# Products of the identity in TensorE's idle stretches between the first projections and the experts

## The chip, the cores and the metric

The kernel runs on one core of a Trainium2 chip. The metric is the device time of one execution in microseconds (us). The engines are PE (TensorE: PE for its matmuls, PEld for its weight loads), DVE (VectorE), ACT (ScalarE), POOL (GpSimd) and SP (SyncE, which issues most of the DMAs).

## The reference, cut to what matters

The network has two blocks over 512 tokens of width 1024, all in float32. The first block ends in a mixture of experts: each token takes one of 4 groups, and 2 of the 8 experts of that group.

```python
g_logits = (t @ w_group + b_group)                     # 512 x 4
e_logits = einsum('td,gde->tge', t, w_expert) + b_expert   # 512 x 4 x 8
e_sel = e_logits of the group with the largest g_logit
top_vals, top_idx = lax.top_k(e_sel, 2)
gate = softmax(top_vals) * softmax(g_logits)[group]
act = silu(t @ w_gate_up[g, e, :, :256]) * (t @ w_gate_up[g, e, :, 256:])
y = sum over the chosen experts of gate * act @ w_down[g, e]
```

Ahead of it stand a projection (`proj = h @ w_in`), a causal attention, a spatial gating (`z = w_spatial @ layer_norm(gelu(vs))`) and an output projection with a layer norm. The second block (retention, state space, latent attention, two feed-forward layers) isn't touched.

## The kernel before, in words

Each engine has one program, a list of stages in fixed order (`tensor`, `scalar`, `vector`, `gpsimd`, `sync` at the end of `program`). Nothing is planned at run time: an engine runs its instructions in the order written and waits on semaphores (`wait_ge`) for what it needs from the others. TensorE's stages that matter here are `proj1_pe`, `attn1_pe`, `out1_pe`, `route_pe` and `experts_pe`, in this order. All matrices are cut in four blocks of 128 tokens, t = 0 to 3.

- `proj1_pe` (L642) makes the first projection with `proj3`, three products of rounded parts for each block, and near its end the spatial gating: `spatial(t)` is 8 products of a 128x128 matrix with 128x64 columns (`each`, L141), after `ln_dve` on DVE has made `vs_norm` of that block. At the end it makes the first scores of the attention (`scores1(p, 0)`), then `spatial(3)`; `attn1_pe` starts when DVE has used all four (`gated`).
- `out1_pe` (L867) is the output projection, 16 column groups of 8 products. Between these it takes each finished block: `turn(t)` makes 8 transposes (`turns`, L147) of the normalised rows, once DVE has made them (`h1`); ACT copies them to SBUF (`h1_T_copy`); `logits(t)` is 8 products with 36 columns (`acc`, L135). For the last blocks nothing is left to do between, so the order is `logits(2)`, `turn(3)`, `logits(3)`.
- `route_pe` (L978) sorts the tokens to experts. `route_dve` works out the choice in a chain of small instructions and raises `chosen`. TensorE then counts ranks (L982, L984: `ranks`), DVE works out the places (`selected`), TensorE makes the row numbers with 8 products of 48 columns (L135: `row_ids`), DVE converts them (`token_ids`), and POOL gathers the rows of the first tile by an indirect DMA (L1189).
- `experts_pe` (L1202 on) runs over 24 tiles of work: `rows(j)` makes 8 transposes of the gathered rows, which ACT and DVE copy; `up(j)` is 16 products of 512 columns (L1216), `down(j)` 8 (L1229). SP fetches the weights of tile n when tile n-2's `up` and `down` have freed their place (`expert_piece`, L1117 on, its DMAs at L1130): those of the first two tiles are there before, and the next fetch waits for the end of `up(0)`.

A semaphore is raised by the last product of a group, and what stands behind it in TensorE's list doesn't hold it back. PSUM has 8 banks; `bk(i, n)` is the first n columns of bank i.

Of the kernel before, what the change touches and what calls it, by code (L numbers as in the profile page):

```python
# [224 lines left out]
def program(nc, A, out):  # L225
    S = Sems(nc, FOLLOWS)
# [7 lines left out]
    def bk(i, n=512, at_=0):  # L234
        return PS[:, 512 * i + at_:512 * i + at_ + n]
# [23 lines left out]
    ident, ones, iot = C["ident"], C["ones"], C["iot"]  # L259
# [125 lines left out]
    def landed(x, n):  # L385

        x.wait_ge(S(f"piece{U[n]['slot']}"), U[n]["turn"])
        return cut(U[n], U[n]["raw"])
# [87 lines left out]
    def ada_pe(p, c):  # L476
        if c < 24:
            w, b, q = ada_weights(p, c), ada_bank(c // 12), c % 12
            p.wait_ge(S("bcol"), 1)
            for i in range(2):  # L480
                for j in range(4):
                    k = 2 * j + i
                    ins = p.e.matmul(PS[32 * j:32 * j + 32, 512 * b:512 * b + 512], cTv[:, k, 22 - 2 * q:54 - 2 * q], w[k // 4][:, k % 4, :],
                                     start=q == 0 and i == 0, stop=q == 11 and i == 1)
            p.up(ins, S("ada_row"))
        if c in (12, 24):
            p.wait_ge(S("ada_copy"), c // 12)
            p.each([(bk(ada_bank(c // 12 - 1), 24, 24 * b), arow[:, 128 * b:128 * b + 128], sel24[:, 0:24]) for b in range(4)], S("ada_T"))
# [137 lines left out]
    def proj3(p, n, t, bank, aH_, aL_, inc):  # L626
        wh, wl = parts(p, n)
        ts_ = slice(128 * t, 128 * t + 128)
        p.acc(bk(bank, 256), three([(aH_[:, k, ts_], aL_[:, k, ts_]) for k in range(8)],
                                   [(wh[:, k, :], wl[:, k, :]) for k in range(8)]), inc=inc)  # L630

    SCORE = (0, 1, 2, 7)

    def scores1(p, n):
        for m in (n, n + 1):
            h, t = units1[m]
            r0 = 64 * (h % 2)
            p.wait_ge(S("masked"), m - 3)
            p.each([(bk(SCORE[m % 4], 128 * t + 128), qT[r0:r0 + 64, h // 2, 128 * t:128 * t + 128],
                     kT[r0:r0 + 64, h // 2, 0:128 * t + 128])], inc=S("score"))  # L640

    def proj1_pe(p):  # L642
        p.wait_ge(S("x_low"), 8)

        def turn(i):
            p.wait_ge(S("roped1"), i + 1)
            p.wait_ge(S("qkT_copy"), i - 1)
            x = tmp[i % 2][:, 0:256]
            p.turns([(bk(6 + i % 2, 128, 128 * b), x[:, 128 * b:128 * b + 128]) for b in range(2)], ident, S("qk_T"))

        def spatial(t):
            p.wait_ge(S("vs_norm"), t + 1)
            p.wait_ge(S("gated"), t - 1)
            p.each([(bk(6 + t % 2, 64, 64 * g), wspT[:, g, :], vst[:, t, 64 * g:64 * g + 64]) for g in range(8)], inc=S("spatial"))

        for n in range(10):
            for t in range(4):
                g = 4 * n + t
                if g >= 4:
                    p.wait_ge(*((S("v_copy"), g - 3) if g < 12 else (S("act1"), g - 11)))  # L660
                proj3(p, W_IN[n], t, g % 4, xH, xL, S("proj1"))
                if n < 8 and t % 2:
                    ada_pe(p, g // 2)
                if 17 <= g < 33:
                    turn(g - 17)
                if g == 33:
                    p.wait_ge(S("wsp_m"), 1)
                    p.wait_ge(S("qkT_copy"), 16)
                    for h in range(2):
                        p.turns([(bk(6 + h, 128, 128 * j), wsp[:, 4 * h + j, :]) for j in range(4)], ident, S("wsp_T"))  # L670
                    p.wait_ge(S("wsp_copy"), 1)
                    p.turns([(bk(6, 8), X[0:8, 512:640])], ident, S("wsp_T"))
                    p.wait_ge(S("wsp_copy"), 3)
                if n == 9 and t:
                    spatial(t - 1)

        p.wait_ge(S("act1"), 31)
        scores1(p, 0)
        spatial(3)

    def proj1_act(a):
# [117 lines left out]
    def attn1_dve(v):  # L799
        c = 16  # L800
        for n in range(35):
            if n < 32:
# [5 lines left out]
                v.settle()  # L808
                v.stt(x[:, 0:w], bk(SCORE[n % 4], w), 0.125, lnc[:, t, 0:w], ALU.mult, ALU.add, inc=S("masked"))
                v.settle()  # L810
# [56 lines left out]
    def out1_pe(p):  # L867
        ada_pe(p, 24)
        p.wait_ge(S("o_copy"), 4)
        p.wait_ge(S("prob_T_copy"), 32)  # L870
        for k in range(4):
            p.wait_ge(S("mix_T_copy"), k - 2)
            p.turns([(bk((3, 5, 6)[k % 3], 128, 128 * t), mix1[:, t, 128 * k:128 * k + 128]) for t in range(4)], ident, S("mix_T"))
        p.wait_ge(S("mix_T_copy"), 4)

        def turn(t):
            p.wait_ge(S("h1"), t + 1)
            for b in range(2):
                p.wait_ge(S("h1_T_copy"), 2 * t + b - 1)
                p.turns([(bk(5 + b, 128, 128 * j), hl[:, t, 128 * (4 * b + j):128 * (4 * b + j) + 128]) for j in range(4)],  # L880
                        ident, S("h1_T"))

        def logits(t):
            p.wait_ge(S("h1_T_copy"), 2 * t + 2)
            p.wait_ge(S("logit"), t - 1)
            p.wait_ge(S("in3"), 176)
            p.acc(bk(3 + t % 2, 36), [(hT[:, k, 128 * t:128 * t + 128], wr[:, k, :]) for k in range(8)], inc=S("logit_m"))

        for c in range(2):
            w = [landed(p, W_O + 2 * c), landed(p, W_O + 2 * c + 1)]  # L890
            for t in range(4):
                g = 4 * c + t
                p.wait_ge(S("added1"), g - 2)
                p.acc(bk(g % 3), [(mT[:, k, 128 * t:128 * t + 128], w[k // 4][:, k % 4, :]) for k in range(8)], inc=S("out1"))
                if c and t >= 2:
                    logits(t - 2)
                if c and t:
                    turn(t - 1)
        logits(2)
        turn(3)  # L900
        logits(3)

    def out1_act(a):
        for k in range(4):
            a.wait_ge(S("mix_T"), k + 1)
            a.cast(mT[:, 4 + k, :], bk((3, 5, 6)[k % 3]), inc=S("mix_T_copy"))

        def copies(t):
            for b in range(2):
                a.wait_ge(S("h1_T"), 2 * t + b + 1)  # L910
                a.cast(hT[:, 4 * b:4 * b + 4, 128 * t:128 * t + 128], bk(5 + b).rearrange("p (k t) -> p k t", k=4), inc=S("h1_T_copy"))

        for t in range(4):
            if t:
                copies(t - 1)
            ln_act(a, LNS1)
        copies(3)
# [60 lines left out]
    def route_pe(p):  # L978

        p.wait_ge(S("chosen"), 1)  # L980
        tile = lambda q, n: v32(AS)[:, q, :].unsqueeze(1).to_broadcast([P, n, 32])
        p.e.matmul(bk(0, 160), C["U"], AS5, start=True, stop=False)  # L982
        for q in range(4):
            ins = p.e.matmul(bk(0, 160).rearrange("p (t n) -> p t n", t=5)[:, q + 1:5, :], ones, tile(q, 4 - q),  # L984
                             start=False, stop=q == 3)
        p.up(ins, S("ranks"))
        p.wait_ge(S("selected"), 1)
        p.acc(bk(1, 48), sel, inc=S("row_ids"))

    def route_act(a):  # L990
        answer(a, ge, ge, ACT.Exp)
        answer(a, dd, dd, ACT.Exp)
# [1582 lines left out]
    for l in range(2):  # L2575
        n = 0
# [393 lines left out]
    def tensor(e):  # L2970
        p = Lane(e, S("own_pe"))
        begin_pe(p)
        proj1_pe(p)
        attn1_pe(p)
        out1_pe(p)
        route_pe(p)
        experts_pe(p)
        qkv_pe(p)
        ret_pe(p)
        gnorm_pe(p)  # L2980
        conv_pe(p)
        ssd_pe(p)
        mix_pe(p)
        p.wait_ge(S("mixed_T_copy"), 16)
        ffn_pe(p, 0, aT, RWO, next_pe)
        latent_pe(p)
        heads_pe(p, 0)
        heads_pe(p, 1)
        p.wait_ge(S("o2_copy"), 32)
        p.wait_ge(S("exp2"), 64)  # L2990
        ffn_pe(p, 1, oT, MWO, nothing)
# [112 lines left out]
```

## Time and profile before

| | us |
|---|---|
| median of 3 runs | 2585.84 |
| the 3 runs | 2596.91, 2581.55, 2585.84 |
| time of the profiled execution | 2584.93 |
| its span in the trace | 2583.1 |
| TensorE's matmuls busy | 2427.2 |
| TensorE's weight loads busy | 1714.6 |
| DVE busy | 1144.3 |

The time of the profiled execution is its span and 1.8 us around it. All times in the rows below are microseconds from the start of the span, unless ns is written. A busy TensorE is one with a matmul under way, at whatever clock.

### The profile page before, as it was taken

The page shows a single profiled execution, that of the slowest core. Times are in us where ns is not written, and L with a number is a line of the kernel's source. Part 1 is how long each engine was busy: PE and PEld are TensorE (multiplying, and loading weights), DVE is VectorE, ACT ScalarE, POOL GpSimd, SP SyncE. Part 2 cuts the span into 40 slices and gives each one's busy share as a digit, 9 for nine tenths or more (in the row PEclk, how much of TensorE's full clock was granted, in tenths as well). Part 3 has the DMA queues.
Part 4 walks back from the last instruction along what each step waited for, and adds up shares of the span by engine and source line. Part 5 has one row for each costly group of instructions (what it writes and reads, how often), then busy time and mean ns, then how long its engine had stood idle before and what let it go on. Part 6 is the DMA issues. An engine that isn't in the chain of part 4 may idle for free.

```text
span 2583.1 us, 29977 instructions
## 1 busy us (share of the span) xinstructions
PE 2427.2 (94%) x12470; PEld 1714.6 (66%) x12470; DVE 1144.3 (44%) x1952; ACT 691.6 (27%) x1215; POOL 153.4 (6%) x147
## 2 busy tenths in 40 slices
PE   8998969999999998899999999999988999999998
PEld 6783433333445887747888888877756554788886
DVE  3247332111464666735443433443264473544444
ACT  2235012111133333314112112122253352322222
POOL 0000011111104104200000000000000000000000
PEclk9999969999999999999999999999999999999999
DMA  9937649998411510122112212112200101322222
GB/s 340 358 128 262 237 160 379 334 362 321 160 26 35 66 49 1 68 96 66 50 49 82 66 49 82 66 33 84 66 17 1 66 1 33 98 80 94 94 94 79
DMA packets 180039, 305.65 MB, mean 118 GB/s; under 512 B 18315, under 2 KB 89787, under 8 KB 179776
## 3 DMA queue, kind: packets, MB, share of 16 engines
q1 hardware_dynamic: 167792, 278.40, 31.8%
q0 software_dynamic: 11376, 23.17, 2.7%
q8 instruction: 99, 1.62, 0.3%
q10 hardware_dynamic: 736, 2.15, 0.2%
q14 instruction: 36, 0.29, 0.0%
HBM read 351.90 MB, written 18.90 MB: 144 GB/s over the span
## 4 chain that ended last, share of the span: by engine, by line
PE 61%; DVE 7%; ACT 3%; issue 2%; POOL 0%; DMA 0%; DVEq 0%; ACTq 0%
PE PS L135 37%; PE PS L2430 11%; PE PS L2374 4%; PE PS L141 3%; PE PS L147 3%; PE PS L2840 2%; DVE sm L116 1%; DVE X L105 1%; DVE H L105 1%; PE PS L2317 1%; DVE rest L105 1%; DVE MIX L105 1%; ACT ATb L128 1%; DVE H L113 1%; DVE R L113 0%
## 5 line engine op out<-in xcount | busy, mean ns | idle before, releaser
L135 PE MATMUL PS<-at,wH 128*128 128x512 f32 (+1 forms) x2144 | 563.2, 352 | 2.1 <-DVE at L105 2.1
L135 PEld LDWEIGHTS PS<-at,wH 128*128 128x128 f32 x2144 | 378.2, 189 | 56.9 <-DVE at L105 2.3
L135 PE MATMUL PS<-at,rest 128*128 128x512 f32 (+1 forms) x1072 | 376.3, 351 | 0.0
L2430 PE MATMUL PS<-wH,ac 128*128 128x512 f32 x880 | 277.8, 393 | 3.3 <-DVE hn L105 3.3
L105 DVE TENSOR_TENSOR rest<-ring,wH 128x2048 fp32r<-128x2048 f32 x66 | 150.4, 2291 | 211.1 <-ACT wH L128 210.5
L135 PEld LDWEIGHTS PS<-at,rest 128*128 128x128 f32 x1072 | 202.7, 189 | 27.0
L128 ACT CAST wH<-ring 128x2048 fp32r<-128x2048 f32 x66 | 124.6, 1906 | 272.1 <-PE PS L2430 199.8
L2430 PEld LDWEIGHTS PS<-wH,ac 128*128 128x128 f32 x880 | 165.2, 188 | 42.9 <-DVE hn L105 8.4
L2430 PE MATMUL PS<-rest,ac 128*128 128x512 f32 x440 | 171.4, 389 | 0.0
L135 PE MATMUL PS<-HI,ATr 128*128 128x256 f32 x512 | 150.0, 293 | 4.8 <-DVE MIXr L105 4.0
L135 PE MATMUL PS<-ring,AT 128*128 128x512 f32 x320 | 141.6, 599 | 0.8 <-ACT AT L128 0.8
L105 DVE TENSOR_TENSOR hn<-PS,gate 128x512 f32<-128x512 f32 x120 | 83.0, 692 | 104.4 <-PE PS L2430 99.3
L141 PE MATMUL PS<-R 96*128 96x256 f32 (+6 forms) x344 | 113.0, 488 | 14.9 <-DVE X L105 10.1
L105 DVE TENSOR_TENSOR sil<-sil,PS 128x512 f32<-128x512 f32 x66 | 39.5, 599 | 171.9 <-PE PS L135 171.8
L135 PEld LDWEIGHTS PS<-HI,ATr 128*128 128x128 f32 x512 | 100.3, 196 | 15.6 <-issue 10.8
L128 ACT COPY R<-PS 128x256 f32<-128x256 f32 (+4 forms) x148 | 65.6, 459 | 167.9 <-PE PS L135 139.1
L135 PEld LDWEIGHTS PS<-ring,AT 128*128 128x128 f32 x320 | 60.4, 192 | 74.2 <-issue 73.1
L135 PE MATMUL PS<-ring,X 128*128 128x256 f32 (+1 forms) x384 | 106.5, 433 | 1.3 <-ACT MIXb L128 1.3
L105 DVE TENSOR_TENSOR MIX<-MIX,PS 128x256 f32<-128x256 f32 (+1 forms) x34 | 15.9, 469 | 206.2 <-ACT MIX L125 205.3
L128 ACT CAST ac<-sil 128x1536 fp32r<-128x1536 f32 (+1 forms) x22 | 27.8, 1265 | 295.1 <-DVE sil L105 295.1
L2430 PEld LDWEIGHTS PS<-rest,ac 128*128 128x128 f32 x440 | 82.7, 188 | 17.0 <-issue 0.7
L147 PEld LDWEIGHTS PS<-con,R 128*128 128x128 f32 (+1 forms) x512 | 57.2, 137 | 55.0 <-issue 28.6
(332 smaller groups left out, 3896.7 us busy)
## 6 DMA issues: line engine op xcount, KB each, us to landing
R<-in_w_gate_up_dram SPq DMA_DIRECT2D x32, 1024.0 KB, 12.0
ring<-in_w_down_dram SPq DMA_DIRECT2D x32, 1024.0 KB, 12.6
ring<-in_w_gate_up_dram SPq DMA_DIRECT2D x32, 1024.0 KB
ring<-in_w_ffn_gate_dram SPq DMA_DIRECT2D x22, 1024.0 KB, 5.4
ring<-in_w_ffn_up_dram SPq DMA_DIRECT2D x22, 1024.0 KB, 5.5
ring<-in_w_ffn_down_dram SPq DMA_DIRECT2D x22, 1024.0 KB, 5.0
ring<-in_w_ada_dram SPq DMA_DIRECT2D x16, 1024.0 KB, 7.5
HIw<-in_w_gate_up_dram SPq DMA_DIRECT2D x16, 1024.0 KB, 8.7
```

The costliest lines, as they stand in the source:

```text
L105: return self.up(self.e.tensor_tensor(dst, a, b, op), inc)
L113: return self.up(self.e.scalar_tensor_tensor(dst, a, s, b, op0, op1), inc)
L116: return self.up(self.e.tensor_reduce(dst, a, AX, op, negate=neg), inc)
L128: return self.up(self.e.copy(dst, src), inc)
L135: ins = self.e.matmul(out, l, r, start=k == 0, stop=k == len(pairs) - 1)
L141: ins = self.e.matmul(o, l, r, start=True, stop=True)
L147: ins = self.e.transpose(o, i_, ident[0:i_.shape[0], 0:i_.shape[0]])
L2317: p.e.matmul(bk(t), aT[:, k, 128 * t:128 * t + 128], w[:, k, :], start=k == 0, stop=False)
L2374: ins = p.e.matmul(bk(g % 4), oT_[:, k, 128 * t:128 * t + 128], w[k // 4][:, k % 4, :], start=k == 0, stop=k == 7)
L2430: ins = p.e.matmul(bk(4 + n_dn % 3), a_, b_, start=start and i == 0, stop=stop and i == len(terms) - 1)
L2840: ins = p.e.matmul(PS[64 * e:64 * e + 64, 512 * 6:512 * 6 + 256], vm[:, b, 64 * h:64 * h + 64], pTm[b // 3][:, b % 3, 256 * e:256 * e + 25 ...
```

## The change

A function `keep_busy(p, b, n)` issues n products of the 128x128 identity with itself, to the first 128 columns of bank b. Nobody reads them, they raise no semaphore, and the only wait that comes with them is that for `ada_add` at the first place, which guards bank 5. It is called at six places: 18 products between the first scores and `spatial(3)`; 14 between `logits(2)` and `turn(3)`; 5 between `turn(3)` and `logits(3)`; 44 behind `logits(3)`, ahead of the wait for `chosen`; 60 behind the ranks, ahead of the wait for `selected`; 44 behind the row numbers, ahead of the experts' first transposes. That is 185 products.

```diff
+    def keep_busy(p, b, n):
+
+        for _ in range(n):
+            p.e.matmul(bk(b, 128), ident, ident, start=True, stop=True)
...
         p.wait_ge(S("act1"), 31)
         scores1(p, 0)
+        p.wait_ge(S("ada_add"), 1)
+        keep_busy(p, 5, 18)
         spatial(3)
...
         logits(2)
+        keep_busy(p, 7, 14)
         turn(3)
+        keep_busy(p, 7, 5)
         logits(3)
+        keep_busy(p, 7, 44)
...
         p.up(ins, S("ranks"))
+        keep_busy(p, 7, 60)
         p.wait_ge(S("selected"), 1)
         p.acc(bk(1, 48), sel, inc=S("row_ids"))
+        keep_busy(p, 7, 44)
```

## Rows read from the trace of the kernel before

**Rows 1.** The page, busy time of TensorE, and its granted clock in 40 slices

```profile
PE 2427.2 (94%) x12470; PEld 1714.6 (66%) x12470; DVE 1144.3 (44%) x1952; ACT 691.6 (27%) x1215; POOL 153.4 (6%) x147
PEclk9999969999999999999999999999999999999999
```

**Rows 2.** Timeline of TensorE from the third block's logits to the experts' first products

```profile
320.42 1.98 PE L135 MATMUL PS<-X,MIX 128*128 128x36 f32 x16 [0.72 <-ACT MIX L128]
...
324.09 1.97 PE L147 MATMUL PS<-con,H 128*128 128x128 f32 x8 [1.70 <-DVE H L105]
...
326.73 3.63 PE L135 MATMUL PS<-X,MIX 128*128 128x36 f32 x16 [0.67 <-ACT MIX L128]
...
335.90 0.90 PE L982 MATMUL PS<-MIX,con 128*128 128x160 f32 x2 [5.53 <-DVE MIX L105]
...
345.78 3.65 PE L135 MATMUL PS<-X,MIX 128*128 128x48 f32 x16 [7.43 <-DVE X L105]
...
354.78 1.94 PE L147 MATMUL PS<-con,MIX 128*128 128x128 f32 x8 [5.35 <-DMA MIX<-h1d,sm]
...
357.55 6.51 PE L1216 MATMUL PS<-HIw,AT 128*64 128x512 f32 x16 [0.83 <-issue]
```

**Rows 3.** Stretches of 1 us and one of 5: busy time of engines, granted clock (PEclk)

```profile
core 0: us, PE busy (x) PEld busy (x) DVE busy (x) ACT busy (x) POOL busy (x), PEclk, DMA share, GB/s
...
322.00:323.00 1.00, 0.39 (x4) 0.28 (x3) 0.97 (x2) 0.00 (x0) 0.00 (x0) 0.69 0.00 0
323.00:324.00 1.00, 0.00 (x0) 0.00 (x0) 1.00 (x2) 0.00 (x0) 0.00 (x0) 0.50 0.00 0
...
362.00:363.00 1.00, 1.00 (x6) 0.37 (x4) 0.00 (x0) 0.00 (x0) 0.00 (x0) 0.50 0.00 0
363.00:364.00 1.00, 1.00 (x6) 0.28 (x4) 0.00 (x0) 0.00 (x0) 0.00 (x0) 0.83 0.00 0
...
175.00:180.00 5.00, 5.00 (x33) 5.00 (x31) 3.28 (x5) 1.24 (x2) 0.00 (x0) 0.66 0.00 0
```

**Rows 4.** Timeline: what DVE and POOL start on TensorE's results

```profile
338.38 0.19 DVE L110 TENSOR_SCALAR MIX<-PS 128x32 f32<-128x32 f32 x1 [1.13 <-PE PS L984]
...
349.46 0.21 DVE L109 TENSOR_SCALAR sm<-PS 128x48 uint32<-128x48 f32 x1 [1.58 <-PE PS L135]
...
350.56 1.09 POOL L1189 DMA_INDIRECT MIX<-h1d,sm  x1 [17.18 <-DVE sm L109]
```

**Rows 5.** Timeline: what SP issues when up(0) and up(1) end

```profile
367.53 0.92 SPq L1130 DMA_DIRECT2D HIw<-in_w_gate_up_dram  x2
...
376.47 1.80 SPq L1130 DMA_DIRECT2D R<-in_w_gate_up_dram  x3
```

**Rows 6.** Timeline: the like instructions at the full clock

```profile
316.92 1.87 PE L135 MATMUL PS<-X,MIX 128*128 128x36 f32 x16
...
318.62 1.07 PE L147 MATMUL PS<-con,H 128*128 128x128 f32 x8
...
319.29 1.07 ACT L128 COPY MIX<-PS 128x512 f32<-128x512 f32 x2 [8.31 <-PE PS L147]
...
369.35 4.05 PE L1216 MATMUL PS<-R,AT 128*64 128x512 f32 x17 [0.48 <-issue]
```

**Rows 7.** Timeline of the weight loads of float32 products in a later stage, full clock

```profile
846.82 1.87 PEld L1798 LDWEIGHTS PS<-ring,X 128*128 128x128 f32 x16
848.61 1.87 PEld L1795 LDWEIGHTS PS<-R,X 128*128 128x128 f32 x16
```

**Rows 8.** Timeline of TensorE and DVE at the end of the first projections

```profile
186.08 0.49 PE L141 MATMUL PS<-R 64*128 64x128 f32 x4
...
189.17 3.62 PE L141 MATMUL PS<-R,X 128*128 128x64 f32 x16 [2.60 <-DVE R L105]
...
192.83 0.69 DVE L105 TENSOR_TENSOR R<-PS,X 128x512 f32<-128x512 f32 x1 [2.19 <-PE PS L141]
...
194.35 2.71 PE L141 MATMUL PS<-R 64*128 64x256 f32 x8 [1.56 <-issue]
```

**Rows 9.** Two stretches of the experts, columns as in rows 3

```profile
370.00:390.00 20.00, 20.00 (x100) 7.76 (x98) 2.23 (x4) 1.56 (x3) 3.33 (x4) 1.00 1.04 384
610.00:630.00 20.00, 18.85 (x91) 6.79 (x89) 3.06 (x6) 1.94 (x4) 2.00 (x2) 1.00 1.03 392
```

## The prediction

> **What bounds the kernel now.** I read the page first: TensorE's matmuls are busy for 94% of the span, and its granted clock stands at 9, the highest digit of the page, in 39 of 40 slices; only the sixth (323 to 388 us) stands at 6 [rows 1]. That is the slice of the routing. So the change can only work on one short stretch, and I went there with the windows of 1 us. The clock falls within 322 to 323 us, and stands at 0.50, which is 1.2 GHz, in forty windows one after the other, from 323 to 363; within 363 to 364 it comes back [rows 3]. In that stretch the timeline of TensorE shows six pieces of work with four large holes: 1.70 us before the last transposes, 5.53 before the ranks, 7.43 before the row numbers, 5.35 before the experts' first transposes, and a small one of 0.67 before the last logits [rows 2]. Each hole ends on DVE, ACT or a gather, each of which began on TensorE's product before it: this is one chain in which TensorE's pieces, at half clock, and the others' pieces take turns. DVE starts on the ranks at 338.38 and on the row numbers at 349.46, and POOL gathers at 350.56 [rows 4]. Behind the chain SP's next fetches of weights start at 367.53, when up(0) has ended, and the following ones at 376.47, after up(1) [rows 5]. From there TensorE is busy 19 to 20 of 20 us and the DMA engines are at 1.03 to 1.04, at the start as at the end of the experts [rows 9]. Neither has room to catch up, and nothing can be fetched earlier, so what up(0)'s end moves by, the end of the kernel moves by. The sum below is that one number.
>
> **What the clock costs now.** Last logits 3.63 us against 1.87 at the full clock; transposes 1.97 and 1.94 against 1.07 [rows 2, 6]. The ranks take 338.38 - 335.90 = 2.48 and would take 1.25. up(0), from 357.55 to 367.53, takes 9.98, up(1) from 369.35 to 376.47 takes 7.12 [rows 2, 5, 6]. All of it together is worth some 9 us. That is the most the change could give, if the products fitted in the holes.
>
> **The price of one product.** An acc of 8 float32 products shows as 16 matmuls, 8 transposes show as 8 [rows 2]: a float32 product is two records, a transpose one. So each product of keep_busy is two records too, both with a 128x128 weight load. No product of the identity with itself is in the trace. The nearest row is a float32 product of the same shape (128x128 with 128 columns) at the full clock: 16 records start between 846.82 and 848.61, which is 1.79 us for 8 products, 0.224 us each [rows 7]. The narrower ones are no cheaper: 1.87 to 1.98 for 8 with 36 columns, 0.24 each [rows 2, 6]. From below I bound it at 0.12 us, if it were one record like a transpose (8 in 1.07, which start some 0.12 apart) [rows 6]; from above at 0.44, the price at half clock (3.63 for 8, less the tail of the last) [rows 2]. I take 0.224, the row with the same operands' shape. Then 5 products are 1.12 us, 18 are 4.03, 44 are 9.86 and 60 are 13.4. The holes are 0.67, 2.60, 5.53 or 5.35, and 7.43 [rows 2, 8]. Every filling is longer than its hole, nearly by a factor of two. Since TensorE runs its list in order, what is queued behind the products (the transposes, the ranks, the row numbers) waits for them, and DVE, ACT, POOL and SP wait for that.
>
> A rule of the Trainium skill bears on this price: "FP8 and Floating Point Precision", section TensorE Precision Notes, says that a true float32 product passes the array four times. As an estimate from that page, 4 times 128 columns at 2.4 GHz is 0.213 us, and the sum below would fall by some 1.8 us; the 0.12 of a single record would not be reachable.
>
> **The steps.** Start at 322.40, the end of logits(2) (320.42 + 1.98). The clock falls there on account of what TensorE did before, and nothing of that is changed, so I let it fall. How long it stays down under unbroken matmuls a dip earlier in the kernel shows: 175 to 180 us, TensorE busy for all 5 us, clock 0.66, so 5 x 0.34 / 0.5 = 3.4 us at half [rows 3]. In 3.4 us at 0.44 there go 7.7 of the 14 products, the other 6.3 take 1.4 us: 4.8 in all. The bounds are 3.1 (no dip) and 6.2 (all at half).
> 1. turn(3) starts at 327.2 and not at 324.09; it takes 1.07 and not 1.97: 328.3.
> 2. Five products: 329.4. Without them the logits could start 1.80 us after the transposes' start (320.42 - 318.62, where ACT's two copies lie between), at 329.0 [rows 2, 6]. The products decide, by 0.4.
> 3. logits(3), 1.9 at the full clock: 331.3. Before, it was 326.73 + 3.63 = 330.36. Late by 0.9: the faster clock has nearly paid for the 14 products.
> 4. 44 products until 341.2. DVE has chosen 5.54 us after the logits (335.90 - 330.36), at 336.8. Overshoot 4.4. Ranks 1.25: 342.4, and not 338.38. Late by 4.0.
> 5. 60 products until 355.8. DVE needs 345.78 - 338.38 = 7.40: it is done at 349.8. Overshoot 6.0. Row numbers 1.9: 357.7, and not 349.43. Late by 8.3.
> 6. 44 products until 367.6. The gathered rows are there 5.35 later, at 363.1. Overshoot 4.5. Transposes and copies take 2.0 at the full clock (the 1.80 above, and 0.2 since here DVE's later copy counts too), and not 2.77: up(0) starts at 369.6, and not 357.55. Late by 12.0.
> 7. up(0) 7.1 and not 10.0: it ends at 376.7, and not 367.53. Late by 9.2.
>
> At the first place: the scores end at 186.57, 18 products take until 190.6, spatial(3) starts then and not at 189.17, but at 1.87 and not 3.62 [rows 7, 8]. It ends at 192.5 where DVE started on it at 192.83: 0.3 us earlier. The wait for ada_add is for something made long before, and costs nothing. Attention behind it begins on DVE's and ACT's turns; its first scores (2.71 us at half clock [rows 8]) are not what DVE waits for, so I count no further gain; bounds 0 and 1.5 us. If the clock didn't hold, cover is gone here too, and this place costs 5.3 us (rival 2).
>
> Sum: 9.2 - 0.3 = 8.9 us. On the profiled execution's own time, 2584.93, this is 2593.8. The median of the runs is 0.9 above that execution: 2594.7. The bounds of the price (0.213 to 0.24) and of the dip (3.1 to 6.2) move it by -3.5 to +4.0 us, the first place by -1.2.
>
> **Rivals.**
> 1. The products fit (not slower than before). One product is one record, 0.12 us, at the holes' places: 14 are 1.7, 44 are 5.3, 60 are 7.2, 44 are 5.3, all but a trifle below the holes of 1.70, 5.53, 7.43, 5.35. For it speaks that the fillings match the holes so well at this price; against it that each plain float32 product in the trace is two records. By the same steps: the 14 run in the dip (3.1), turn(3) starts at 325.5, logits(3) ends at 329.3, ranks at 336.1, row numbers at 345.4, up(0) starts at 352.7 and ends at 359.8. That is 7.7 earlier, with the 0.3 above 8.0: 2577.8. It turns on the price alone: by the steps, at about 0.17 us each the change neither gains nor loses.
> 2. The clock isn't held, since products of the identity, most of whose terms are zero, may not count for the throttle. Then each costs 0.44 and all the rest stays at half clock: 14 are 6.2, turn and 5 products 4.2, logits(3) ends at 336.4; 44 are 19.4, ranks end at 358.3; 60 are 26.4, row numbers end at 388.3; 44 are 19.4, up(0) starts at 410.4 and ends at 420.4, 52.9 late; at the first place 18 are 7.9 and spatial(3) ends 5.3 late. In all 58.2: 2644.0. For it: right before the clock fell, TensorE was transposing by the identity and making narrow products, busy for most of the time [rows 2, 6], so being busy isn't the whole of it. Against it: plain float32 products hold 1.00 through the experts [rows 9].
>
> The Trainium skill, "TensorE: Matmul & The Clock Gate", section Part 4: PE-mode transpose, says that a transpose doesn't count as TensorE being busy in the same way. Were the added products counted as that page has transposes counted, rival 2 would hold; they are plain products by the diff, so I weigh this low.
>
> **How the numbers follow.** The forecast 0.78, rival 1 0.15, rival 2 0.05, 0.02 for anything else. The likeliest alone is 2588 to 2603 with the spread of a median. The three runs of before lie 15 us apart, so the range is widened at the top to 2604; below, it takes in rival 1: 2577 to 2604. A measurement of this kernel tells about 1% (26 us) from no change. The forecast (+0.34%) and rival 1 (-0.31%) are both within it: 0.93. Slower by over 1% is rival 2 and a little more: 0.06. Faster by over 1% would need 26 us, where half clock costs 9: 0.01.
>
> **What would show it.** In the profile after: matmuls of the identity with itself, 370 of them, at about 0.11 us from one to the next; at the places of the holes no idle time on TensorE, and the ranks, the row numbers and the experts' first transposes starting 4.4, 6.0 and 4.5 us later than what they wait for is ready; granted clock 1.00 from about 326 us on; up(1) starting some 10 us after 369; the experts as long as before. One record for each product, or holes that remain before the ranks, would prove rival 1; clock 0.50 with TensorE busy, rival 2. I would be wrong also if the experts' stage became shorter by what its start is late.

## The result, and the profile after

| | before | after |
|---|---|---|
| median, us | 2586.47 (20 runs) | 2595.56 (20 runs) |
| lowest and highest, us | 2581.55, 2598.74 | 2592.28, 2605.47 |
| ratio, with its 95% interval | | 1.0036 (1.0024 to 1.0048) |
| time of the profiled execution, us | 2584.93 | 2603.31 |
| its span, us | 2583.1 | 2601.5 |

The change makes the kernel 0.36% slower: 9.1 us of medians, where 8.9 were forecast, and 2595.56 us where 2594.7 were. A measurement can tell this from nothing only because there are 20 runs of each.

First the page of the kernel after, its busy times and the granted clock in 40 slices, to hold against [rows 1]:

```profile
PE 2469.2 (95%) x12840; PEld 1754.6 (67%) x12840; DVE 1143.1 (44%) x1952; ACT 691.3 (27%) x1215; POOL 153.5 (6%) x147
PEclk9999999999999999999999999999999999999999
```

TensorE is busy for 42 us more, has 370 matmuls and 370 weight loads more, and the one slice with a 6 is gone. Whoever read only the clock would call this a success. Next, all instructions of the added line (L635, the product in `keep_busy`): count, form, and shortest, median and longest duration in ns:

```profile
L635 PEld LDWEIGHTS PS<-con x370: 186/192/334, 186.2 to 366.1; 128*128 128x128 f32 x185
L635 PE MATMUL PS<-con x370: 274/275/422, 186.2 to 366.2; 128*128 128x128 f32 x185
```

185 products are 370 matmuls, as read from [rows 2]. The line that would name who waited for them is empty: nobody reads them. What they cost stands in the timeline of TensorE over the same stretch as [rows 2], with the SP row that answers to [rows 5]:

```profile
319.87 1.97 PE L135 MATMUL PS<-X,MIX 128*128 128x36 f32 x16 [0.73 <-ACT MIX L128]
321.67 5.00 PE L635 MATMUL PS<-con 128*128 128x128 f32 x28
...
326.51 1.04 PE L147 MATMUL PS<-con,H 128*128 128x128 f32 x8
...
327.38 1.28 PE L635 MATMUL PS<-con 128*128 128x128 f32 x10
...
328.50 1.87 PE L135 MATMUL PS<-X,MIX 128*128 128x36 f32 x16
...
330.20 10.07 PE L635 MATMUL PS<-con 128*128 128x128 f32 x88
...
340.11 0.44 PE L992 MATMUL PS<-MIX,con 128*128 128x160 f32 x2
...
341.20 13.64 PE L635 MATMUL PS<-con 128*128 128x128 f32 x120
...
354.68 1.88 PE L135 MATMUL PS<-X,MIX 128*128 128x48 f32 x16
...
356.40 10.05 PE L635 MATMUL PS<-con 128*128 128x128 f32 x88
...
366.29 1.04 PE L147 MATMUL PS<-con,MIX 128*128 128x128 f32 x8
...
368.15 3.65 PE L1228 MATMUL PS<-HIw,AT 128*64 128x512 f32 x16 [0.83 <-ACT AT L128]
...
375.27 0.92 SPq L1142 DMA_DIRECT2D HIw<-in_w_gate_up_dram  x2
...
377.10 4.05 PE L1228 MATMUL PS<-R,AT 128*64 128x512 f32 x17 [0.49 <-issue]
```

No row has an idle time in brackets from 321.67 to 366.29: every hole of [rows 2] is full. The 44, 60 and 44 products take 9.91 us (330.20 to 340.11), 13.48 (341.20 to 354.68) and 9.89 (356.40 to 366.29), so 0.225 us each. The pieces between are as fast as hoped: logits 1.87, row numbers 1.88, transposes 1.04, up(0) 7.12 (368.15 to 375.27) and not 9.98. What waited is seen on DVE and POOL:

```profile
341.40 0.19 DVE L110 TENSOR_SCALAR MIX<-PS 128x32 f32<-128x32 f32 x1 [4.12 <-PE PS L994]
...
356.60 0.21 DVE L109 TENSOR_SCALAR sm<-PS 128x48 uint32<-128x48 f32 x1 [5.72 <-PE PS L135]
...
357.69 1.09 POOL L1201 DMA_INDIRECT MIX<-h1d,sm  x1 [24.30 <-DVE sm L109]
```

DVE's last instruction before the ranks ended at 337.27, and it sat idle for 4.12 us until they came, where that was 1.13 in [rows 4]. Before the row numbers it was 5.72 and not 1.58. The granted clock in stretches of 1 us, as in [rows 3]:

```profile
322.00:323.00 1.00, 1.00 (x8) 1.00 (x7) 0.96 (x2) 0.00 (x0) 0.00 (x0) 0.55 0.09 16
...
325.00:326.00 1.00, 1.00 (x9) 1.00 (x8) 0.00 (x0) 0.00 (x0) 0.00 (x0) 0.74 0.19 55
326.00:327.00 1.00, 1.00 (x12) 1.00 (x11) 0.00 (x0) 0.00 (x0) 0.00 (x0) 1.00 0.99 358
...
366.00:367.00 1.00, 1.00 (x12) 1.00 (x11) 0.00 (x0) 0.07 (x1) 0.00 (x0) 1.00 0.00 0
```

It falls at the end of logits(2) as before, comes back within 325 to 326 after some 3.4 us of products at half clock, and stays at 1.00.

The profiled execution is 18.4 us longer in span than that of before, twice the change of the medians. Up to the start of up(1) it is 7.75 us later (377.10 against 369.35); the other 10.7 us come behind. Read in stretches of 10 us, the clock was at half for some 61 us between up(1) and the end in this execution, and for 34 us in that of before. A view by stretches of 20 us in the last attention shows a part of the difference, with the columns of [rows 3], first before, then after (the same times aren't the same work, since the kernel after is some 8 us behind):

```profile
1980.00:2000.00 20.00, 19.16 (x97) 16.52 (x94) 3.10 (x9) 3.62 (x9) 0.00 (x0) 1.00 0.00 1
...
2140.00:2160.00 20.00, 18.46 (x65) 8.98 (x64) 3.06 (x5) 1.21 (x3) 0.00 (x0) 1.00 0.00 1
```

```profile
1980.00:2000.00 20.00, 16.25 (x91) 11.46 (x88) 5.11 (x11) 5.61 (x13) 0.00 (x0) 0.83 0.00 1
...
2140.00:2160.00 20.00, 16.13 (x91) 10.20 (x91) 11.73 (x24) 8.60 (x19) 0.00 (x0) 0.88 0.00 0
```

The clock falls there in this execution and not in the other; from 1860 to 2180 us that of before is at 1.00 throughout, and this one below it in six of sixteen such stretches. From the start of up(1) to the end of the span the twelve kernels of this text, whose code is the same there, took 2213.8 us (before) to 2224.4 us (after) in their profiled executions. For the effect of an edit I therefore read a stretch that ends at the start of up(1), not the whole span.

### The profile page after: what moved, and what is told of

It reads as the page before. It is cut to its first block, busy times and chain, and to the rows that moved or that the text cites. A ratio compares the mean times of both kernels' runs of the same rounds, so it can differ in the third digit from the quotient of the medians.

```text
span 2601.5 us, 30717 instructions
## 1 busy us (share of the span) xinstructions
PE 2469.2 (95%) x12840; PEld 1754.6 (67%) x12840; DVE 1143.1 (44%) x1952; ACT 691.3 (27%) x1215; POOL 153.5 (6%) x147
## 4 chain that ended last, share of the span: by engine, by line
PE 61%; DVE 7%; ACT 3%; issue 2%; DMA 0%; DVEq 0%; ACTq 0%; POOL 0%
PE PS L135 37%; PE PS L2442 10%; PE PS L2386 4%; PE PS L141 3%; PE PS L147 3%; PE PS L2852 2%; DVE sm L116 1%; DVE X L105 1%; DVE H L105 1%; PE PS L2329 1%; DVE rest L105 1%; DVE MIX L105 1%; DVE H L113 0%; ACT R L125 0%; ACT ATb L128 0%
```

## The experiments

Each kernel is read by one number besides its time: **the stretch**, from the end of logits(2) to the start of up(1). Before it is 369.35 - 322.40 = 46.95 us, after it 377.10 - 321.84 = 55.26 us. It leaves out what lies ahead of it: the gain of the first place, and up to 0.43 us in e2, e7 and e8, where the clock falls within logits(2), which then takes 2.41, 2.41 and 2.31 us and not 1.98.

| kernel | stretch, us | expected | median, us | ratio to before, 95% |
|---|---|---|---|---|
| before | 46.95 | | 2586.47 | |
| after | 55.26 | | 2595.56 | 1.0036 (1.0024 to 1.0048) |
| e1_fit | 39.63 | 39.3 | 2582.49 | 0.9972 (0.9959 to 0.9985) |
| e2_transposes | 39.86 | 39 or 65 | 2578.72 | 0.9966 (0.9950 to 0.9982) |
| e3_first_only | 46.84 | 47 | 2586.49 (1 run) | |
| e4_sixty_doubled | 68.66 | 68.9 | 2616.18 (1 run) | |
| e5_fit_and_before | 38.35 | 38.2 or 39.6 | 2577.81 | 0.9963 (0.9949 to 0.9976) |
| e6_last_only | 42.58 | 43.5 to 44.1 | 2579.15 (1 run) | |
| e7_no_last | 42.67 | 43.3 or 39.6 | 2580.42 (1 run) | |
| e8_half_full | 38.13 | 39, or 41 to 46 | 2579.30 (1 run) | |
| e9_half_and_before | 39.93 | 37 to 38.5, or up to 40 | 2581.10 | 0.9979 (0.9965 to 0.9994) |
| e10_before_only | 44.93 | 45 to 47, or 40 | 2585.21 (1 run) | |

The single times say little, since 20 runs of one kernel lie 17 us apart; of those kernels only the stretch is used.

### The counts that fit: e1_fit

```diff
-        keep_busy(p, 5, 18)
+        keep_busy(p, 5, 11)
-        keep_busy(p, 7, 14)
+        keep_busy(p, 7, 7)
-        keep_busy(p, 7, 5)
+        keep_busy(p, 7, 2)
-        keep_busy(p, 7, 44)
+        keep_busy(p, 7, 23)
-        keep_busy(p, 7, 60)
+        keep_busy(p, 7, 31)
-        keep_busy(p, 7, 44)
+        keep_busy(p, 7, 23)
```

> The counts cut to what the holes hold at 0.228 us a product: 11, 7, 2, 23, 31, 23 in place of 18, 14, 5, 44, 60, 44. I read the time from the end of logits(2) to the start of up(1): 46.95 us before, 55.26 with the change. Theory (the change is slow because its products are longer than the holes): no product is waited for any more but those that fall in the 3.4 us dip, the clock is at 1.00 from about 325 us on, and the stretch is 39.3 us, so 7.7 less than before; with the 0.3 of the first place the time is some 8 us under the kernel before (ratio 0.997). Rival (it isn't the overshoot but what the products bring with them, such as dips of the clock in later stages): the stretch may shrink, but the time stays above the kernel before.

Measured: stretch 39.63, ratio 0.9972. The sign turns with nothing changed but the counts. The timeline of TensorE in this kernel:

```profile
331.82 0.54 PE L992 MATMUL PS<-MIX,con 128*128 128x160 f32 x2 [0.34 <-DVE MIX L105]
...
340.67 1.99 PE L135 MATMUL PS<-X,MIX 128*128 128x48 f32 x16 [0.50 <-DVE X L105]
...
348.26 1.06 PE L147 MATMUL PS<-con,MIX 128*128 128x128 f32 x8 [0.40 <-DMA MIX<-h1d,sm]
...
357.27 0.92 SPq L1142 DMA_DIRECT2D HIw<-in_w_gate_up_dram  x2
```

Small holes are left before the ranks (0.34), the row numbers (0.50) and the transposes (0.40), ended by DVE and by the gather: the products end before what comes next is ready, and the clock is held all the same (1.00 in every stretch of 3 us from 324 on). The rival, that the products harm by what they bring with them, falls.

### A price times a count: e4_sixty_doubled

```diff
-        keep_busy(p, 7, 60)
+        keep_busy(p, 7, 120)
```

> The 60 products behind the ranks are doubled to 120, all else as in the change. Theory (each product behind a hole's end costs its full price on the one chain): the stretch from the end of logits(2) to the start of up(1) grows by 60 x 0.227 = 13.6 us, from 55.3 to 68.9, and the experts end as much later. Rival (the experts' stage takes up part of a late start): the end of the experts moves by clearly less than 13.6.

Measured: stretch 68.66, which is 13.40 more than with 60, so 0.223 us for each added product. The experts keep the delay: their last `down` products begin at 686.4 us here and at 672.4 in the kernel after, which is 295.3 us behind the start of up(1) in both, as in the kernel before (664.7). The rival falls.

### Transposes in place of products: e2_transposes

```diff
-            p.e.matmul(bk(b, 128), ident, ident, start=True, stop=True)
+            p.e.transpose(bk(b, 128), ident, ident)
```

> The same 185 instructions, each a transpose of the identity in place of a product: one record each, about 0.12 us at the full clock and 0.23 at half, so they fit the holes if the clock is held. Theory A (transposes hold the clock as products do): stretch from the end of logits(2) to the start of up(1) some 39 us, time about 8 us under the kernel before. Theory B (transposes don't count for the throttle as products do, as the Trainium skill's page TensorE: Matmul & The Clock Gate has it): granted clock 0.50 from 322 us into up(0) though TensorE is busy throughout, the transposes overshoot the holes at half clock, stretch about 65 us, time about 18 us above the kernel before.

Measured: stretch 39.86, ratio 0.9966: theory A. The same counts that are too many as products fit as transposes, which are one record of 0.11 us (60 in 6.75). This is the price that rival 1 gave to the products. The clock, in stretches of 3 us, with the columns of [rows 3]:

```profile
321.00:324.00 3.00, 2.82 (x23) 2.58 (x21) 0.00 (x0) 1.41 (x3) 0.35 (x1) 0.88 0.61 171
324.00:327.00 3.00, 3.00 (x29) 3.00 (x29) 1.08 (x7) 0.94 (x1) 1.03 (x2) 1.00 0.97 336
...
339.00:342.00 3.00, 2.09 (x19) 1.94 (x18) 2.76 (x9) 0.00 (x0) 0.00 (x0) 1.00 0.02 5
342.00:345.00 3.00, 3.00 (x17) 3.00 (x16) 1.66 (x10) 1.80 (x4) 1.81 (x2) 0.53 0.03 5
345.00:348.00 3.00, 3.00 (x27) 3.00 (x26) 0.00 (x0) 2.41 (x3) 2.12 (x3) 0.90 0.88 283
```

It comes back within 321 to 324 and once more within 345 to 348, each time while TensorE did transposes alone. In between it fell once, at about 342, behind a stretch with 0.91 us of idle time before the row numbers (TensorE busy 2.09 of 3 us) and the row numbers themselves, 8 products of 48 columns. That dip lay under the 44 transposes and cost some 0.7 us: from the row numbers to the experts' transposes it is 8.31 us (340.07 to 348.38), and 7.59 in e1_fit. In e1_fit, with products and 0.50 us idle at the same place, the clock didn't fall; whether the transposes or the longer idle time made the difference wasn't tested. Under the transposes themselves the clock stood at 1.00 from 325.5 to 330.5 and from 332.4 to 339.2, and it rose from 0.50. The Trainium skill says in "TensorE: Matmul & The Clock Gate", section Part 4: PE-mode transpose, that a transpose doesn't count as TensorE being busy in the same way, and that the full clock doesn't engage for it. This trace doesn't agree, and the measurement decides.

### The first place alone: e3_first_only

```diff
-        keep_busy(p, 7, 14)
-        keep_busy(p, 7, 5)
-        keep_busy(p, 7, 44)
-        keep_busy(p, 7, 60)
-        keep_busy(p, 7, 44)
```

> Only the 18 products at the first place; the five other places are taken out. By my steps this place is worth 0.3 us: logits(2) end 0.3 us earlier than in the kernel before, the stretch from there to up(1) is 47 us as before with the clock at 0.50, and the time is the kernel before's within what one run tells. Rival (the clock kept in the attention's first part speeds up the attention): logits(2) end 1.5 us earlier or more.

Measured: stretch 46.84, as before. Its logits(2) end at 320.56 and not at 322.40, which is more than the 0.3 expected and reaches the rival's 1.5. But the same number is 322.47 in e4_sixty_doubled, which has the same 18 products and nothing else ahead of logits(2), and it is 320.30 in e6_last_only, which has none. What sets it is another dip: between 250 and 255 us the clock is at 0.66 in the executions of before, after, e4 and e10, which all end logits(2) between 321.8 and 322.5, and at 1.00 in e3 and e6, which end it at 320.3 to 320.6. So the rival isn't shown, and what the first place is worth can't be read from this number. Inside one execution the place itself can: spatial(3) starts when the 18 products end and takes 1.90 us, as this timeline of the kernel after shows, to hold against [rows 8]:

```profile
185.79 0.49 PE L141 MATMUL PS<-R 64*128 64x128 f32 x4
...
186.21 4.29 PE L635 MATMUL PS<-con 128*128 128x128 f32 x36
...
190.33 1.90 PE L141 MATMUL PS<-R,X 128*128 128x64 f32 x16
...
192.26 0.69 DVE L105 TENSOR_TENSOR R<-PS,X 128x512 f32<-128x512 f32 x1 [1.91 <-PE PS L141]
```

From the start of the scores to DVE's work on spatial(3) it is 6.47 us (185.79 to 192.26) and was 6.75 (186.08 to 192.83): 0.28 gained. The fitted count does better here too. In e1_fit, with 11 products:

```profile
184.74 0.49 PE L141 MATMUL PS<-R 64*128 64x128 f32 x4
...
187.84 2.00 PE L141 MATMUL PS<-R,X 128*128 128x64 f32 x16
...
189.88 0.69 DVE L105 TENSOR_TENSOR R<-PS,X 128x512 f32<-128x512 f32 x1 [0.57 <-PE PS L141]
```

That is 5.14 us, 1.6 less than before, and with 5 products (e8_half_full, e9_half_and_before) it is 5.13. The stretch doesn't hold this gain. The 18 products were too many by some 1.3 us.

### The last place alone: e6_last_only

```diff
-        keep_busy(p, 5, 18)
-        keep_busy(p, 7, 14)
-        keep_busy(p, 7, 5)
-        keep_busy(p, 7, 44)
-        keep_busy(p, 7, 60)
         p.acc(bk(1, 48), sel, inc=S("row_ids"))
-        keep_busy(p, 7, 44)
+        keep_busy(p, 7, 12)
```

> 12 products at the last place alone, ahead of the experts' first transposes; at half clock these take 5.3 us, which is the hole. All else as in the kernel before. Theory (the long up(0) at half clock is the largest single part of the gain, and one place of busy TensorE right ahead of it is enough): ranks and logits as slow as before, but the granted clock rises to 1.00 by the first transposes and up(0) takes 7.1 and not 10.0 us, stretch from the end of logits(2) to up(1) 43.5 to 44.1 us against 46.95 before. Rival (the clock comes back only after longer work): up(0) at half for part of its time, stretch 45 or more.

Measured: stretch 42.58, 4.4 us less than before, more than the 2.9 to 3.4 expected. Two rows of TensorE's timeline:

```profile
346.30 5.01 PE L635 MATMUL PS<-con 128*128 128x128 f32 x24
...
352.05 1.06 PE L147 MATMUL PS<-con,MIX 128*128 128x128 f32 x8 [0.74 <-DMA MIX<-h1d,sm]
```

The 12 products take 5.01 us, mostly at half clock; then the clock is up, and the transposes too run at full (1.06 and not 1.94). Some 0.9 us of the 4.4 isn't theirs: in this execution the clock fell only after turn(3), which took 1.09. From the start of the row numbers to up(1) it is 20.03 us (342.85 to 362.88) and was 23.57 (345.78 to 369.35): 3.5 us by 12 products. Up to 1.2 us of this may be chance: in e10_before_only (below), which has no products at this place either, the same distance is 22.39 us, because the clock came back earlier within up(0). So the 12 products are worth 2.4 to 3.5 us.

### All but the last place: e7_no_last

Against e1_fit:

```diff
         p.acc(bk(1, 48), sel, inc=S("row_ids"))
-        keep_busy(p, 7, 23)
```

> The fitted counts without those of the last place. Theory: the clock falls in the 5.35 us in which the rows are gathered; the transposes (1.9 and not 1.1) and up(0) (10.0 and not 7.1) pay for it: stretch 39.6 + 0.8 + 2.9 = 43.3 us. Rival (once held up to there, the clock outlasts the hole): stretch 39.6.

Measured: stretch 42.67, 3.04 more than e1_fit. The timeline shows the bill, to hold against the last rows of e1_fit:

```profile
347.17 1.94 PE L147 MATMUL PS<-con,MIX 128*128 128x128 f32 x8 [5.46 <-DMA MIX<-h1d,sm]
...
349.94 6.36 PE L1227 MATMUL PS<-HIw,AT 128*64 128x512 f32 x16 [0.83 <-issue]
...
359.77 0.92 SPq L1141 DMA_DIRECT2D HIw<-in_w_gate_up_dram  x2
```

The clock fell in the hole of 5.46 us; transposes 1.94, up(0) 9.83 (349.94 to 359.77). It doesn't outlast the hole. From the start of logits(2), which took 0.43 us longer here, the two kernels differ by 3.47 us, near the 3.7 expected.

### Ahead of the fall: e5_fit_and_before

Against e1_fit:

```diff
+        keep_busy(p, 7, 3)
         logits(2)
```

> The fitted counts, and 3 products more in the idle 0.72 us ahead of logits(2), which comes before the clock falls. With the fitted counts the stretch from the end of logits(2) to the start of up(1) is 39.6 us; in it the clock is still at half for 3.4 us right behind logits(2). Theory A (the clock falls there because of the hole ahead of logits(2)): it no longer falls, 7 products take 1.6 and not 2.7 us, the transposes 1.1 and not 1.7, stretch 38.2, and the time is 1.4 us less than with the fitted counts alone. Theory B (it falls because transposes and products of 36 columns are too thin, the hole being only a small part): it falls all the same, stretch 39.6.

Measured: stretch 38.35, ratio 0.9963, theory A. The clock is at 1.00 in every stretch of 2 us from 312 to 378; two of them, around the end of logits(2), with the columns of [rows 3]:

```profile
316.00:318.00 2.00, 1.94 (x18) 1.89 (x17) 1.73 (x3) 0.16 (x2) 0.00 (x0) 1.00 0.00 0
318.00:320.00 2.00, 1.95 (x17) 1.76 (x17) 1.90 (x4) 0.00 (x0) 0.00 (x0) 1.00 0.00 0
```

The beginning of its timeline:

```profile
315.23 0.83 PE L635 MATMUL PS<-con 128*128 128x128 f32 x6
...
316.12 1.98 PE L135 MATMUL PS<-X,MIX 128*128 128x36 f32 x16
...
317.92 1.81 PE L635 MATMUL PS<-con 128*128 128x128 f32 x14
...
319.78 1.09 PE L147 MATMUL PS<-con,H 128*128 128x128 f32 x8
```

7 products take 1.8 us here and 2.7 in e1_fit, and the transposes 1.09 and not 1.68. That the time is lower than e1_fit's isn't established: the intervals of the two ratios overlap. In the three profiled executions with the 3 products in the hole of 0.72 us (this one, and those of e9 and e10 below) the clock held through logits(2) and turn(3). In the nine without them it fell within logits(2) or less than 0.5 us behind it in eight; in e6_last_only it fell some 3 us later. So they seem to help, but twelve executions don't show it for sure, nor that the hole alone decides.

### Half-full holes: e8_half_full and e9_half_and_before

Of e8_half_full, against the change; e9_half_and_before is the same with `keep_busy(p, 7, 3)` ahead of logits(2):

```diff
-        keep_busy(p, 5, 18)
+        keep_busy(p, 5, 5)
-        keep_busy(p, 7, 14)
+        keep_busy(p, 7, 3)
-        keep_busy(p, 7, 5)
+        keep_busy(p, 7, 1)
-        keep_busy(p, 7, 44)
+        keep_busy(p, 7, 12)
-        keep_busy(p, 7, 60)
+        keep_busy(p, 7, 16)
-        keep_busy(p, 7, 44)
+        keep_busy(p, 7, 12)
```

> Half of the fitted counts: 5, 3, 1, 12, 16, 12, so each hole begins with products and ends idle. Theory A (half a hole of work keeps the clock up): 1.00 between 326 us and up(0), stretch about 39 us, as with the fitted counts. Theory B (it doesn't): the clock falls in one or more of the three long holes and the pieces behind it run at half; stretch between 41 and 46 us.

Measured: stretch 38.13. The clock did fall, within logits(2) (2.31 us) and once more within 330 to 332, behind the ranks and the hole before them, of which 2.79 us were idle. It was back by 334: the 16 products that stood there took 5.44 us and not the 3.82 of e9_half_and_before, and had room for it in a hole of 7.4. So the second fall cost the chain nothing, which neither theory had. That 38.13 is below the 38.35 of e5 is no gain: the stretch begins at the end of logits(2), and here 0.3 us of the first dip lie within logits(2) (2.31 and not 1.98).

> Half of the fitted counts (5, 3, 1, 12, 16, 12) and 3 products ahead of logits(2). With the fitted counts and the 3 products the stretch from the end of logits(2) to the start of up(1) was 38.4 us and the clock never fell in it; with half the counts alone it fell right in logits(2) and once in the hole before the row numbers, stretch 38.1. Theory (half a hole of work is enough, and the hole ahead of logits(2) is what lets the clock fall there): no fall at logits(2), stretch 37 to 38.5, time as with the fitted counts and the 3 products, 8 to 10 us under the kernel before. Rival (with so little work the clock falls by the chance of where the idle part lies): a fall of 3.4 us in one of the long holes, stretch up to 40.

Measured: stretch 39.93, ratio 0.9979; the rival. At logits(2) the clock held. The next fall came later than in e8_half_full, as two rows of TensorE's timeline show:

```profile
330.74 3.82 PE L635 MATMUL PS<-con 128*128 128x128 f32 x32
...
338.40 3.64 PE L135 MATMUL PS<-X,MIX 128*128 128x48 f32 x16 [3.85 <-DVE X L105]
```

TensorE was idle for 3.85 us before the row numbers, and these ran at half: 3.64 us and not 1.99. In these two executions it was chance whether a dip lies under products that have room or under the work. That e9's ratio is above e5's isn't established; their intervals overlap.

### The three products alone: e10_before_only

Against the kernel before (with the helper of the change):

```diff
+        keep_busy(p, 7, 3)
         logits(2)
```

> Only the 3 products ahead of logits(2), nothing else. Theory (the throttle looks at what lies just behind): the clock holds through logits(2), but falls in the holes that follow, by 327 us at the latest; the ranks, row numbers and up(0) at half as in the kernel before, stretch 45 to 47 us. Rival (what counts is that one moment): clock at 1.00 further on and the stretch near 40.

Measured: stretch 44.93. The clock held through logits(2) and turn(3) (1.09 us), fell in 325 to 326, and was at 0.50 into up(0). The rival falls, and the theory's course of the clock was met. But e6_last_only, with nothing ahead of logits(2), lost the clock at the same point, ahead of logits(3), so this run by itself doesn't show what the 3 products did. The 2.0 us less than before have two sources: the transposes of turn(3) at the full clock (0.9), and the clock's return at 360, where it was 363 to 364 in [rows 3]:

```profile
358.00:360.00 2.00, 2.00 (x7) 0.57 (x5) 0.00 (x0) 0.00 (x0) 0.00 (x0) 0.50 0.49 131
360.00:362.00 2.00, 2.00 (x12) 0.74 (x10) 0.00 (x0) 0.00 (x0) 0.00 (x0) 1.00 0.00 0
```

up(0) ran at half for 3.1 us here and for 6.1 in the kernel before, and took 8.6 us (356.89 to 365.53) and not 9.98. The code from turn(3) on is the same in both, so what the half clock costs in up(0) differs by 1.3 us between two executions of it.

The version with the lowest ratio is e5_fit_and_before: the change with 11, 7, 2, 23, 31, 23 products and 3 ahead of logits(2), 0.37% faster than the kernel before, where the change is 0.36% slower. Its chain is 8.6 us shorter behind logits(2) and 1.6 us at the first place. Its interval overlaps those of e1_fit, e2_transposes and e9_half_and_before.

## Why the prediction was right

- **The bound.** Right: one chain from logits(2) to up(0), and what up(0)'s end moves by, the kernel moves by. e4_sixty_doubled has the chain 13.4 us longer, and its experts take as long from up(1) on as before (295.3 us to the last `down`). That the experts can't catch up was read from TensorE at 19 to 20 of 20 us and DMA at 1.03 [rows 9].
- **The price of a product.** The step that decided. 0.224 us by [rows 7], measured 0.225 in the kernel after and 0.223 by doubling. Rival 1 (0.12) would have turned the sign; its price is real, but it is a transpose's. The estimate from the Trainium skill's page "FP8 and Floating Point Precision" (section TensorE Precision Notes), 0.213, is 0.012 below what was measured.
- **The dip.** Forecast at the end of logits(2), 3.4 us long, 4.8 us for 14 products. Measured 4.84 (321.67 to 326.51). I took it as caused by what TensorE did before; that 3 products ahead of logits(2) were followed by no fall in three executions fits this.
- **The steps.** The 44, 60 and 44 products were put at 9.86, 13.4 and 9.86, and took 9.91, 13.48, 9.89. Ranks 1.25, measured 1.29. up(0) 7.1, measured 7.12. Up to SP's fetch the steps gave 9.2 us; measured from the end of logits(2) it is 8.30 (375.27 - 321.84 = 53.43, and 367.53 - 322.40 = 45.13). The 0.9 too many is one small error made several times: I let the products start when the piece before them had ended (1.9 us after its start), but TensorE issues the next product 1.70 to 1.72 us after the piece's start (328.50 to 330.20, 354.68 to 356.40), the records overlap. The same was made behind the ranks, and the transposes with their copies took 1.86 and not 2.0. With the intervals of before (5.54, 7.40 and 5.35 us) the ranks, the row numbers and the transposes began 4.2, 5.9 and 4.4 us after what they wait for was ready; 4.4, 6.0 and 4.5 were forecast.
- **The first place.** 0.3 us forecast, 0.28 measured. That 18 products overshoot here too, and a fitted count gains 1.6 us, wasn't seen.
- **Rival 2** (the clock isn't held) fell with the clock at 1.00 from 326 us on, and even its variant with transposes fell.
- **The sum.** 8.9 forecast; the medians give 9.1. The traces give less: 8.3 from the end of logits(2), 8.0 with the first place, and 7.75 as it stands between the two profiles. The difference is within what the medians leave open (the interval of the ratio is 3 us to either side). So the mechanism and each term are shown, but that the medians came within 0.2 us of the forecast is luck.

## What to carry to other kernels

Work that only keeps the clock up has a price on the chain as soon as it is longer than the hole: count it in records of the trace (a plain float32 product was two, a transpose one), divide the hole by that, and leave a rest (0.34 to 0.50 us in e1_fit did no harm). The place right before a long piece of work that ran at half clock is worth most for its price: here 12 products before up(0) took 2.4 to 3.5 us off the chain, where e5_fit_and_before took 8.6 us off behind logits(2) with 89, and 1.6 at the first place with 11. The places in between weren't tried one by one. And a fall of the clock is to be met ahead of where it falls: with 3 products ahead of logits(2) it didn't fall there in three executions, and half of the 14 behind it ran in the dip.

## What the runs showed of the hardware that wasn't expected

- While TensorE did transposes alone, the granted clock stayed at 1.00 (332.4 to 339.2 us of e2_transposes) and rose from 0.50 (within 345 to 348).
- These holes need not be full, but then it was chance: with holes half filled the clock fell once in the long holes in each of two executions, once under products with room (e8_half_full, no loss), once under the row numbers (e9_half_and_before, 1.6 us lost).
- The same code from up(1) to the end took 2213.8 to 2224.4 us in twelve executions. In the longest, that of after, the clock was at half for some 61 us of it, in the others for 31 to 45. Within the 20 runs of the kernel after, time and mean granted clock go together (2592.28 us at 0.989, 2605.47 us at 0.982). So dips elsewhere seem to make most of the spread between runs; no experiment moved them.
